# Routing weights by one-hot products, one pass over the experts' U and half of V, and a four-slot weight ring in a streaming encoder layer

## The reference, cut to what matters

```
mod = silu(c) @ w_ada + b_ada               # (9, 2048) @ (2048, 12288)
h   = rms_norm(x, g_pre_mix) * (1 + sc1) + sh1
z   = h @ w_in                              # then gated linear attention, conv branch, projections
x   = x + gt1 * rms_norm(mix, g_post_mix)
h2  = rms_norm(x, g_pre_ffn) * (1 + sc2) + sh2
q   = h2 @ w_pq                             # per token 8 heads x 2 halves x 128
s1, s2 = q[half 0] @ k_sub1.T, q[half 1] @ k_sub2.T      # 128 scores each
v1, i1 = top_k(s1, 16); v2, i2 = top_k(s2, 16)
sc, pos = top_k(v1[:, None] + v2[None, :], 16)           # 16 of 256 pairs
idx = i1 * 128 + i2 at pos;  wts = softmax(sc)           # 8 x 16 = 128 experts of 16384 per token
act = gelu(u_exp[idx] . h2)
f   = sum over the 128 experts of wts * act * v_exp[idx]
y   = x + gt2 * rms_norm(f, g_post_ffn)
```

## Time and profile before

| | us |
|---|---|
| median of three runs | 6031.27 |
| the profiled execution's own time | 6028.78 |
| its span, first to last instruction | 6027.2 |
| adaLN stage | 0 to about 405 |
| untouched stages | about 405 to 3141 |
| routing stage | 3141 to 3549 |
| expert stage, U phase | 3549 to 4684 |
| expert stage, V phase | 4684 to 5968 |
| expert stage, end | 5968 to 6027 |

### The profile page before, as it was taken

One profiled execution on the slowest core, in us unless ns is written; L12 is line 12 of the kernel. 1 busy time (PEld: TensorE's weight loads), 2 busy tenths in 40 slices (PEclk: granted clock), 3 DMA queues, 4 the chain that ended last, 5 costly groups with the idle time before them and its releaser, 6 DMA issues. The chain is left out here.

```text
span 6027.2 us, 61921 instructions
## 1 busy us (share of the span) xinstructions
PE 5001.3 (83%) x22684; PEld 4008.5 (67%) x22684; DVE 3592.5 (60%) x3928; ACT 1584.4 (26%) x1877; POOL 2137.0 (35%) x1607
## 2 busy tenths in 40 slices
PE   6869999999997787988771139999998788888885
PEld 2327788888885434877661139999998666666664
DVE  5652211116673333222316948888777899999998
ACT  5643212222222111122310113333222222232222
POOL 0100000001100331000202767888888555555553
PEclk9999999999998898989895569999999999999998
DMA  8752232223323554433423259999999999999997
GB/s 307 260 193 83 96 103 94 91 97 112 112 71 128 173 192 148 155 108 103 143 106 137 14 180 386 399 391 399 379 365 355 382 394 391 392 393 392 392 393 296
DMA packets 462509, 1402.40 MB, mean 233 GB/s; under 512 B 98621, under 2 KB 188733, under 8 KB 377839
## 3 DMA queue, kind: packets, MB, share of 16 engines
q1 hardware_dynamic: 280692, 728.19, 33.8%
q0 software_dynamic: 154624, 631.94, 28.5%
q10 hardware_dynamic: 27072, 40.91, 1.9%
HBM read 1265.77 MB, written 136.19 MB: 233 GB/s over the span
## 5 line engine op out<-in xcount | busy, mean ns | idle before, releaser
L220 DVE TENSOR_TENSOR w_lo<-w_stage,w_hi 128x2048 fp32r<-128x2048 f32 x248 | 568.9, 2294 | 1407.1 <-ACT w_hi L216 1392.8
L225 PE MATMUL ps<-w_hi,act_hi 128*128 128x512 f32 x3040 | 1195.1, 393 | 41.8 <-DVE act_lo L1000 23.0
L226 PE MATMUL ps<-w_lo,act_hi 128*128 128x512 f32 x3040 | 1189.6, 391 | 0.0
L227 PE MATMUL ps<-w_hi,act_lo 128*128 128x512 f32 x3040 | 1189.1, 391 | 0.0
L216 ACT ACTIVATE w_hi<-w_stage 128x2048 fp32r<-128x2048 f32 x248 | 474.5, 1915 | 1493.5 <-PE ps L227 1435.6
L1679 POOL DMA_INDIRECT d_wT<-wt_all,put_all x384 | 750.9, 1956 | 292.5 <-DVEq L1855 139.4
L2124 DVE SCALAR_TENSOR_TENSOR acc<-v_ring,coef,acc 128x2048 f32<-128x2048 f32 x254 | 802.5, 3159 | 32.3 <-DMA v_ring<-v_exp,idx_all 23.8
L2004 PE MATMUL ps<-act_hi,x_hi 128*128 128x384 f32 x2048 | 690.6, 337 | 149.7 <-DVE x_lo L2129 146.5
L2004 PE MATMUL ps<-x_hi,cx_hi 128*128 128x512 f32 x1536 | 617.8, 402 | 218.9 <-DVE cx_lo L2134 179.1
L2076 ACT ACTIVATE x_hi<-x_stage 128x1024 fp32r<-128x1024 f32 x512 | 541.0, 1057 | 918.9 <-PE ps L2006 519.2
L2129 DVE TENSOR_TENSOR x_lo<-x_stage,x_hi 128x1024 fp32r<-128x1024 f32 x512 | 625.3, 1221 | 202.8 <-ACT x_hi L2076 171.7
(11 more groups left out here) (268 smaller groups left out, 5399.1 us busy)
## 6 DMA issues: line engine op xcount, KB each, us to landing
x_stage<-u_turned SPq DMA_DIRECT2D x256, 512.0 KB
x_stage<-v_exp SPq DMA_DIRECT2D x256, 512.0 KB
w_stage<-w_ada SPq DMA_DIRECT2D x96, 1024.0 KB, 4.9
w_stage<-w_in SPq DMA_DIRECT2D x96, 1024.0 KB, 5.2
gw<-d_g SPq DMA_DIRECT2D x256, 192.0 KB
gw<-d_wT SPq DMA_DIRECT2D x256, 192.0 KB
d_wT<-zero SPq DMA_DIRECT2D x12, 2048.0 KB
d_g<-gob ACTq DMA_DIRECT2D x128, 192.0 KB
```

Of the source, the lines that this page charges most:

```text
L220: dve.tensor_tensor(w_lo[:, q % 2], w_in_st[:, q], w_hi[:, q % 2].bitcast(F32), ALU.subtract).then_inc(w_split, 1)
L225: pe.matmul(out, lhs[0], rhs[0], start=first, stop=False)
L226: pe.matmul(out, lhs[0], rhs[1], start=False, stop=False)
L227: return pe.matmul(out, lhs[1], rhs[0], start=False, stop=last)
```

## The change

Three edits, in three stages.

1. adaLN stage: the same `w_hi` and `w_lo` buffers hold four halves of a quarter in place of two quarters. ACT and DVE split 128x1024 numbers at a time, PE runs 6 matmuls on each, and a split waits for the half four places earlier.
2. Routing stage: no clearing, no scatter, no `put_all`. For tiles 0 to 2, the key numbers and weights of a tile are turned on PE, and for each token two one-hot matrices of 128 slots by 128 keys are made, `one1` by ACT (relu(1 - |key - iota|)) and `one2` by POOL (equal, times the weight). PE multiplies them in float32, four tokens to a PSUM bank, ACT copies the bank into `w_buf`, and SP stores 64 tokens at a time (4 MB in runs of 256 bytes) to `d_w`. The order of ACT, PE and SP is written out.
3. Expert stage: U, coefficients and the first half of V's columns go in one pass of 132 steps; a V item follows its U items four steps later. DVE multiplies the scores by `d_w` (`weigh`), the product stays in SBUF for the first half and is stored in `d_gw` for the second, which reads it back once. 182 of the 256 gathered slots lie in the 132 steps, 74 in the 128 steps of the second pass. There is one `h_row` and one `acc`; the sum of tile 3 goes through `d_f3`.

```diff
-            split_lo(dve, 0, 0)
+            def low_half(n):
+                dve.wait_ge(half_hi, n + 1)
+                q = n // 2 % QPC
+                dve.tensor_tensor(half_of(w_lo, n), w_in_st[:, q, n % 2 * QH:(n % 2 + 1) * QH],
+                                  half_of(w_hi, n).bitcast(F32),
+                                  ALU.subtract).then_inc(w_split if n % 2 else half_lo, 1)
...
+                    if n >= 4:
+                        act.wait_ge(half_used, n - 3)
+                    act.activation(half_of(w_hi, n), w_in_st[:, q, j % 2 * QH:(j % 2 + 1) * QH],
+                                   ACT.Copy).then_inc(half_hi, 1)
...
-            sp.wait_ge(s_zero, 1)
-            flat = d_wT.rearrange("c p n -> c (p n)")
-            for z in range(NZ):
-                sp.dma_start(flat[:, z * 4096:(z + 1) * 4096], zero[:]).then_inc(s_clear, 16)
...
+                for h in range(2):
+                    sp.wait_ge(w_taken, t * NW + (h + 1) * NW // 2)
+                    sp.dma_start(d_w[:, :, t * P + h * P // 2:t * P + (h + 1) * P // 2].rearrange("c p n -> p c n"),
+                                 w_buf[:, h]).then_inc(w_out[h], 16)
...
+                        pool.tensor_scalar(one2[:, G % 2, j], iota, id_t[:, t % 2, 1, n:n + 1], id_t[:, t % 2, 2, n:n + 1],
+                                           ALU.is_equal, ALU.mult).then_inc(s_one2, 1)
...
+            def near(t, g):
+                G = t * NW + g
+                if G >= 2:
+                    act.wait_ge(s_one1, G - 1)
+                for j in range(4):
+                    n = 4 * g + j
+                    act.activation(dist[:, G % 2, j], iota, ACT.Abs, scale=-1.0,
+                                   bias=id_t[:, t % 2, 0, n:n + 1]).then_inc(s_dist, 1)
+                act.wait_ge(s_dist, 4 * G + 4)
+                if G >= 2:
+                    act.wait_ge(w_ready, G - 1)
+                act.activation(one1[:, G % 2], dist[:, G % 2], ACT.Relu, scale=-1.0, bias=1.0).then_inc(s_one1, 1)
...
+            for t in range(ND):
+                act.wait_ge(id_ready, t + 1)
+                act.activation(id_t[:, t % 2].rearrange("p a n -> p (a n)"), ps[:, 5, 0:3 * P], ACT.Copy).then_inc(id_taken, 1)
+                act.wait_ge(id_taken, t + 1)
+                for g in range(NW):
+                    near(t, g)
+                    if g == 2:
+                        scores(t + 1)
+                    if g > 0:
+                        take(t, g - 1)
+                    if g == NW // 2:
+                        turn(t + 2)
+                take(t, NW - 1)
+                weights(t + 1)
+            scores(TT - 1)
+            weights(TT - 1)
...
+            for n in range(STEPS):
+                if n < NKEY:
+                    low(u_item(n, 0))
+                if 2 <= n < NKEY + 2:
+                    weigh(n - 2)
+                gathered(n, 0, 2)
+                if n < NKEY:
+                    low(u_item(n, 1))
+                if 3 <= n < NKEY + 3:
+                    coef_low(n - 3)
+                if n >= LAGV:
+                    low(v_item(n - LAGV))
+                gathered(n, 1, 2)
...
-                pool.tensor_tensor(gob[:, m % 3], gw[:, m % 4, 0], gw[:, m % 4, 1], ALU.mult).then_inc(c_done, 1)
```

More of the change, by code:

```diff
@@ L162, in _build @@
     d_decay = dram("d_decay", (P, DK // P, 2 * TP + STREAMS))
-    d_wT = dram("d_wT", (NKEY, P, DN))
-    d_g = dram("d_g", (NKEY, P, DN))
+    d_w = dram("d_w", (NKEY, P, DN))
+    d_gw = dram("d_gw", (NKEY, P, DN))
+    d_f3 = dram("d_f3", (P, D))
     d_post = d_mod[:, 5 * D:6 * D]
@@ L1670, in _build, with route @@
     wt_all = sb(stack, "wt_all", [P, TT * SLOTS])
-    put_all = sb(stack, "put_all", [P, TT * SLOTS], U32)
     lk = link(None, "dve")
[L1673 to L1687, removed]
+    route(nc, a, stage, sem, sb, kc, ps, (idx_all, wt_all), area, d_q, d_w, lk)
+    experts(nc, a, stage, sem, sb, ps, (idx_all, wt_all), act_hi, act_lo, area, d_post, d_w, d_gw, d_f3, d_x2, d_h2)
+def route(nc, a, stage, sem, sb, kc, ps, route_sb, area, d_q, d_w, lk):
+    idx_all, wt_all = route_sb
     ident = kc[:, K_ID:K_ID + P]
+    iota = kc[:, K_IOTA:K_IOTA + P]
     NH = 2 * PH
+    NW = P // 4
+    half = 4 * TT * KD * P
+    spare = 4 * ND * KD * P
+    at_sb = nc.alloc_sbuf_tensor_at
+    qt = at_sb("qt", [P, NH, P], F32, offset=area + spare)
+    q_t = at_sb("q_t", [P, NH, P], F32, offset=area + spare + 4 * NH * P)
+    hot = at_sb("hot", [P, 2, PH, TOPK, TOPK], F32, offset=area + half + spare)
     with stage() as (st, block):
-        qt = sb(st, "qt", [P, NH, P])
-        q_t = sb(st, "q_t", [P, NH, P])
         keys = sb(st, "keys_sb", [P, 2, NKEY])
@@ L1855, in _, with experts @@
                 dve.sem_inc(route_done, 1)
[L1856 to L1862, removed]
+def experts(nc, a, stage, sem, sb, ps, route_sb, act_hi, act_lo, area, d_post, d_w, d_gw, d_f3, d_x2, d_h2):
+    idx_all, wt_all = route_sb
     half = 4 * TT * KD * P
@@ L1908, in experts @@
         x_rows = [u_ring[:, t % RING] if t < RING else v_ring[:, 0] for t in range(TT)]
[L1909 removed]
+        f_rows = [f_sum[:, t] for t in range(ND)] + [f3[:], acc[:]]
         order = [*GT, *range(ND)]
@@ L2041, in _, with high @@
+            for n in range(STEPS):
+                if n < NKEY:
+                    score(n)
+                if n >= LAGV:
+                    add_up(n - LAGV)
+            for m in range(NKEY, 2 * NKEY):
+                add_up(m)
         @block.scalar
         def _(act):
-            act.sem_inc(gelu_done, 2)
-            act.sem_inc(ev_done, 2 * ND)
+            def high(i):
+                act.wait_ge(st_in[i % 3], 16 * (i // 3 + 1))
+                if i >= DEPTH:
+                    act.wait_ge(pe_used, i - DEPTH + 1)
+                act.activation(w_hi[:, i % DEPTH], stg[:, i % 3], ACT.Copy).then_inc(hi_done, 1)
```

542 lines of the change are left out of this document (313 added, 229 removed).

## The result

Four runs of the changed kernel took 5937.03 to 5962.95 us, median 5949.01; four of the kernel before, taken beside them, 6028.75 to 6057.55, median 6037.24. The ratio is 0.985, with a 95% interval of 0.9815 to 0.9884: 1.5% less, where 3.0% was forecast. The profiled execution has a span of 5950.8 us against 6027.2, 76 less.

A forecast was written before the change was run, and what follows sets the result against it. It took adaLN as bound by its depth-two ring, routing by clearing and the last scatter, U by full transfers, V by transfers and DVE. 6028.8 - 75 + 10 - 115 = 5849, median 5852 us; range 5765 to 5950.

The forecast's parts named there:

- S over 110: Routing stage: S is the time to spread one tile, forecast 85 us; over 110 would make the prediction wrong.
- adaLN ring, -75: adaLN stage: four half-size slots stop the ring from binding, a chunk falling from 15.9 to 12.5 us; -75 us.
- Routing, what goes: Routing stage: clearing and the wait for it go, -60 us; the last scatter, 49 us behind DVE's end, goes too.
- Routing, what comes: Routing stage: ACT's list sets 85 us a tile, POOL's 67 hidden beside it; the stage ends +10 us later.
- The first rival: Routing stage: the store or POOL sets the tile pace, 102 or 118 us; price +51 or +99, chance 0.18.
- The handover: Routing stage, between tiles: Exp, sum, reciprocal, product, transposes and the first group add 9 us to each tile's spread.
- tile 4's turn: Routing stage: the last tile can't be hidden, its scores coming after the third spread; 55.7 us of DVE work.
- two packets a run: Routing stage's weight stores: read-modify-write costing two packets per 256-byte run would make a store take 51 us.
- the rival with table loads: Routing stage, ACT: each group loads tables twice, +246 us, 6098; chance 0.05 together with another stall of that size.
- Experts, -115: Expert stage: 1660 us first pass, 633 second and 8 eviction against 2419, less extra loads; -115 us.
- The loss over PE's pace: Expert stage: 6.5%, from 1135 / 1065 in the U phase; the first pass was taken at 1660 us without scatters.
- the coupling rival: Expert stage, fused pass: late gathers on DVE delay splits and thus PE; price +60 to +80, chance 0.14.

The follow-up runs named there:

- `pool_one_op`: The changed kernel with POOL's one-hot instruction only comparing, without the product by the weight; 5893.12 us, routing stage 433 us.
- `take_plain`: The changed kernel with ACT's copy out of PSUM written in one run, so the weights land in another order; 5948.16 us.
- `route_only`: The kernel before with the new routing stage alone, its experts keeping two phases; 6071.8 us, ratio 1.0059.
- `weigh_pool`: The changed kernel with the first pass's product of scores and weights given back from DVE to POOL; 5951.53 us, ratio 0.9871.

## Why the prediction was right and wrong

The direction was right, and the time lies 1 us inside the upper edge of the range. The prediction's own sign of being wrong, S over 110, came true: S is 118. The steps one by one:

- **adaLN ring, -75.** Measured -65: 13.1 us a chunk where 12.5 was taken, and the end 13.5 was given. PE's weight loads still wait for `w_lo`, 33 us in 33 short pieces. Seven of the 23 distances between additions are at most 11.5 us, about PE's own 11.0; the longest are up to 17.2, so the pieces of the norm between the chunks cost some of them more than the 0.5 to 2 us allowed. Right in kind, small by 10.
- **Routing, what goes.** DVE's first MAX8 starts 17.6 us after the stage's start (forecast 17). The clearing and the scatter tail are gone as said. Right.
- **Routing, what comes: the step that failed.** The forecast had "67 us a tile, hidden beside ACT" for POOL, from "0.52 by halving the latter and adding a start", and let ACT's list set the pace at S = 85. The term that was mis-sized is POOL's instruction. It takes 0.777 us from start to start where DVE is quiet and 0.854 on the mean. A tile goes from 67 us to 118: 33 for the instruction's own length (128 x (0.777 - 0.52)), 10 for the three long ones beside DVE's operations, and 8 for the hole at mid-tile. So POOL isn't hidden beside ACT, it sets S. Halving the row for 128x256 (0.922) was the error in the working. That row has one operation too (a multiplication by a pointer), and `pool_one_op` shows 0.60 for one operation on half the elements: the two points give, as an estimate, a start of 0.28 us and 0.32 for 128 columns. The forecast's 0.52 holds a start of 0.12, and nothing for the second operation, which is worth 0.20 (0.80 against 0.60). That the length depends on the second operation no row before could show.
- **The first rival** (chance 0.18) has POOL at S = 118, price +99, time 5951, and the median is 5949. Its mechanism is the one measured. That the numbers meet is luck: its 118 is 128 x 0.92 and not 128 x 0.854 with a hole, the stage missed by 77 and not by 99 (the handovers are shorter than forecast), and the other 30 us came from adaLN and the experts.
- ACT's group was sized 2.45 and would have been 1.24 + 0.63 + 1.03 = 2.90 less overlaps, 2.63 measured in `pool_one_op`. So even with POOL at 0.52 the stage would have been 433 or so (an estimate from `pool_one_op`), +25 and not +10. The copy was taken at 0.5; writing with a step of 64 numbers it takes 1.03 us, in one run 0.60 (`take_plain`).
- The handover was 5.9 us and not 9, and tile 4's turn is bare as forecast, 57 us in which PE and POOL do nothing.
- The half `w_buf` stores landed in 20.9 us (median of 6). The forecast had 26 to 34, and 51 for two packets a run. So 16384 runs took 20.9 x 16 / 16384 = 20 ns each. By the Trainium skill (DMA: Bandwidth & Descriptors, Specifications) such runs are read, changed and written. No run here shows that by itself; the trace has 4.19 MB / 20.9 us = 201 GB/s, about half of the full stretches' rate, and not a price of two scatter packets.
- Of the rival with table loads: one load of 1.3 us in the whole stage. By the Trainium skill (ScalarE: Activation LUTs, Table sets: the hidden batching unit) abs, relu and copy share every set; the trace agrees.
- **Experts, -115.** Measured -95. The first pass takes 1685 us against 1660, the second with the eviction 629 against 641, and the end after 5882 takes 69 in place of 59 us, since the last gathered rows come after the dense work and `acc` waits up to 2.0 us for each.
  The 25 us of the first pass lie at its ends: its first matmul comes 9 us after the stage's start, and the last four items of V, which no U goes with, take 34 us (5219 to 5253) where PE needs 4 x 4.1 = 16. `acc` is at 2.35, as forecast.
  The loss over PE's pace was taken from a row that says something else: the 1135 us of the U phase hold 15 before the first matmul and 26 after the last, in which PE stood still for the scatters; the matmuls themselves ran 1094 against 1065, 2.7% and not 6.5%. Nor did the forecast say that half of the gain is the scatters'.
  The first pass runs at 376 GB/s, less than the 401 of the U phase alone in `route_only`, with PE busy 1625 of 1685 us. I read this as PE and transfers sharing the pass, so that fewer bytes bring less than their share; no run separates them. Within the pass PE waits 47 us for `x_lo`, below the 100 that would have spoken for the coupling rival.
- One end in the working is mis-added: 6.5% loss and 385 GB/s give 1693 + 644 + 11 = 2348, -71 and not -60.

The sum: 10 + 77 + 20 = 107 us short, less 4 in the untouched stages. The profiled execution, 5952.3 us, lies 103 above the 5849 forecast for it, and the median 97 above 5852.

## What to carry to other kernels

When work is moved to an engine that has only far rows for it, don't halve a row: an instruction of half the size keeps its start, and a second operation has a price; let both ends of that price go through the step that says "hidden". Busy share doesn't tell the bound between two full engines; taking time from each in turn does, for it comes back as waiting on the one that isn't. And when a serial list is broken by moving an item earlier, the new place has to be as early as the data allow, or most of the wait stays. Last, compare stretches that are cut at the same event in each trace and not at the same time: cut at the times of another kernel, a phase seems as long as it was, whatever it did.

## What the hardware showed

- GpSimd's comparison of 128x128 float32 with a pointer took 0.60 us, with a second operation 0.80 (medians); VectorE's took 0.28 and 0.34.
- One such GpSimd instruction in each of the three tiles took 6.71 us. Beside it DVE ran four two-input operations of 128x2048 (2.3 us each) one behind the other, and it ended only in the fourth; the rows of POOL, then of DVE, around 3320 us in the changed kernel:

```profile
L1777 POOL TENSOR_SCALAR one<-kc,id_t x9: 787/790/6713, 3317.5 to 3331.5; 128x128 f32<-128x128 f32 x9
L1945 DVE TENSOR_TENSOR hot<-pf,kc x2: 2280/2352/2425, 3319.4 to 3321.7; 128x2048 f32<-128x2048 f32 x2
```

  It goes the other way as well: DVE's `acc` took 4.07 us beside pairs of POOL products and 2.35 without them, and its `coef` of 128x4, also with two inputs, 2.3 us in place of 0.16. By the Trainium skill (GPSIMD Engine Reference, Specifications) the two share their SBUF interfaces, with contention when DVE has two SBUF inputs; the trace agrees. Who pays varied: in the V phase before DVE's `acc` lost 1.6 us on the mean and POOL's product took 1.05; in `weigh_pool` `acc` lost 0.14 and POOL's product took 1.70. What decides it stays open.
- ACT's Abs of 128x128 with a pointer from SBUF start 0.29 us apart, though each is listed with 0.385; four take 1.24 in all.
- ACT's copy of 128x512 from PSUM took 0.60 us written in one run and 1.03 written with a step of 64 numbers (`take_plain` against the changed kernel).
